# A two-block transformer step on one core: gate columns, row maxima and sums of the second block in another form, the last halves by positions, output by two queues

## What is computed

```python
h = rms_norm(x, norm1_w) * (1.0 + scale) + shift
proj = h @ w_in + b_in
(q, k, v, o, z_a, i_pre, f_pre, u, b_gate, c_gate, z_b, g_a, g_b) = split(proj)
# eight heads: i_pre and f_pre are 8 columns each ("gate columns")
b = cumsum(log_sigmoid(f_pre)); d = b[l] - b[s] + i_pre[s]      # causal
m_row = max(running maximum of d, ...)                          # "row maxima"
scores = (q @ k.T) * dk**-0.5 * exp(d - m_row)
num = scores @ v; den = sum(scores)                             # "sums"
h_a = num / max(|den|, exp(-m_row))
...
x = x + gate * (merged @ w_out)
return rms_norm(x, normf_w)
```

## Time and profile before

| | before |
|---|---|
| median of 3 runs | 2489.23 us (2488.03 to 2490.27) |
| the profiled execution, its own time | 2487.7 us |
| its span | 2485.9 us |
| PE busy | 2379.5 us, 96% |
| VectorE (DVE) busy | 1672.4 us, 67% |
| ScalarE (ACT) busy | 1136.7 us, 46% |
| POOL busy | 93.6 us, 4% |
| mean granted clock of PE | 0.981 |

### The profile page before, as it was taken

One profiled execution on the slowest core, in us unless ns is written; L12 is line 12 of the kernel. 1 busy time (PEld: TensorE's weight loads), 2 busy tenths in 40 slices (PEclk: granted clock), 3 DMA queues, 4 the chain that ended last, 5 costly groups with the idle time before them and its releaser, 6 DMA issues.

```text
span 2485.9 us, 27431 instructions
## 1 busy us (share of the span) xinstructions
PE 2379.5 (96%) x10764; PEld 1965.3 (79%) x10764; DVE 1672.4 (67%) x1807; ACT 1136.7 (46%) x1486; POOL 93.6 (4%) x60
## 2 busy tenths in 40 slices
PE   3689999989999999999979999999999999999997
PEld 3577787868888888888868888888888888888886
DVE  7888898968888888755565455565556555555565
ACT  3345566554444444444463434443445544444453
POOL 1000000001111111200000000000000001000000
PEclk8899999989999999999989999999999999999999
DMA  9978889959899999855544655555566657655553
GB/s 330 356 280 312 273 281 348 348 191 339 322 335 325 331 325 324 293 197 199 193 147 164 200 182 190 180 182 183 195 202 203 208 198 247 208 194 189 189 189 110
DMA packets 255668, 600.52 MB, mean 242 GB/s; under 512 B 12680, under 2 KB 13000, under 8 KB 249024
## 3 DMA queue, kind: packets, MB, share of 16 engines
q1 hardware_dynamic: 252640, 589.48, 68.1%
q0 software_dynamic: 2912, 9.44, 1.2%
HBM read 596.74 MB, written 2.13 MB: 241 GB/s over the span
## 4 chain that ended last, share of the span: by engine, by line
PE 89%; DVE 6%; DMA 2%; ACT 2%; issue 1%; SPq 0%; DVEq 0%; ACTq 0%
PE PS L1185 19%; PE PS L1210 19%; PE PS L1211 18%; PE PS L1216 18%; PE PS L1190 10%; DVE BIAS L1655 3%; DMA RAW<-in_w_in 1%; DVE LO L1637 1%; ACT HI L688 1%; DMA RAW<-in_w_ada 1%; PE PS L1307 1%; PE PS L1570 1%; PE PS L1333 0%; PE PS L1516 0%; PE PS L1199 0%
## 5 line engine op out<-in xcount | busy, mean ns | idle before, releaser
L1637 DVE TENSOR_TENSOR LO<-RAW,HI 128x1024 fp32r<-128x1024 f32 x808 | 1021.0, 1269 | 723.3 <-ACT HI L688 722.3
L688 ACT ACTIVATE HI<-RAW 128x1024 fp32r<-128x1024 f32 x808 | 854.3, 1059 | 1228.7 <-PE PS L1216 738.2
L1210 PE MATMUL PS<-HI,XH 128*128 128x512 f32 x2176 | 868.1, 399 | 11.0 <-ACT HI L688 6.5
L1211 PE MATMUL PS<-HI,XL 128*128 128x512 f32 x2176 | 853.4, 392 | 0.0
L1216 PE MATMUL PS<-LO,XH 128*128 128x512 f32 x2176 | 585.9, 391 | 0.6 <-DVE LO L1637 0.6
L1210 PEld LDWEIGHTS PS<-HI,XH 128*128 128x128 f32 x2176 | 412.0, 189 | 101.7 <-ACT HI L688 11.4
L1216 PEld LDWEIGHTS PS<-LO,XH 128*128 128x128 f32 x2176 | 410.7, 189 | 88.5 <-DVE LO L1637 1.7
L1211 PEld LDWEIGHTS PS<-HI,XL 128*128 128x128 f32 x2176 | 412.1, 189 | 83.1 <-issue 1.0
L1655 DVE SCALAR_TENSOR_TENSOR BIAS<-RAW,CACT,BIAS 128x1024 f32<-128x1024 f32 x270 | 346.4, 1283 | 10.5 <-DMA RAW<-in_w_ada 3.1
L1185 PE MATMUL PS<-HI,XH 128*128 128x512 f32 x1056 | 327.7, 392 | 1.1 <-DVE R L1707 1.1
L1185 PE MATMUL PS<-HI,XL 128*128 128x512 f32 x1056 | 326.1, 390 | 0.0
(11 more groups left out here) (283 smaller groups left out, 994.0 us busy)
## 6 DMA issues: line engine op xcount, KB each, us to landing
RAW<-in_w_in SPq DMA_DIRECT2D x208, 1024.0 KB, 5.1
RAW<-in_w_ada SPq DMA_DIRECT2D x112, 1024.0 KB, 5.8
RAW<-in_w_gate SPq DMA_DIRECT2D x88, 512.0 KB, 4.5
RAW<-in_w_up SPq DMA_DIRECT2D x88, 512.0 KB, 5.5
RAW<-in_w_down SPq DMA_DIRECT2D x44, 1024.0 KB, 4.8
RAW<-in_w_ada SPq DMA_DIRECT2D x64, 512.0 KB, 6.5
RAW<-in_w_out SPq DMA_DIRECT2D x32, 1024.0 KB, 5.3
RAW<-in_w_proj_b SPq DMA_DIRECT2D x16, 1024.0 KB, 5.1
```

The costliest lines, as they stand in the source:

```text
L688: act.activation(HI[:, (it["half"] + hf) % HLS, :], RAW[:, it["slot"], hf * 1024:(hf + 1) * 1024], ACT.Copy).then_inc(s.hi_ready, 1)
L1210: pe.matmul(PS[:, bank + u, :], XH[:, 2 * n + kk, rows], hi, start=start and kk == 0, stop=False)
L1211: pe.matmul(PS[:, bank + u, :], XL[:, 2 * n + kk, rows], hi, start=False, stop=False)
L1637: dve.tensor_tensor(LO[:, slot, :], RAW[:, it["slot"], hf * 1024:(hf + 1) * 1024], HI[:, slot, :].bitcast(F32), ALU.subtract).then_inc(s.l ...
```

## The change

It has five parts, none of which alters the result.

1. Gate columns with operands exchanged: the 16 columns are stationary, 256 positions move, the result lies as rows [16 x 256]. The bias is added per partition by VectorE into ROWG, PE's turn goes, and rows 8 to 15 reach partitions 0 to 7 by a DMA of POOL. VectorE waits for it in `gate_rows_out`.
2. Row maxima: ROWM goes to DRAM, and eight broadcasts of POOL's queue bring each row to all partitions (MAXB); the product with SEL and the load of SEL go.
3. Sums: V2 holds 257 columns per head, the last of them ones, so that the same product gives the sum; the product with ones goes.
4. The last two halves take the first positions through both, then the second; `leave` and the squares follow position by position; the first positions' output goes in two pieces by SP, the second's by ScalarE's queue, and the norm's weight is multiplied in ahead of the root.
5. Small loads: positions and frequencies behind the first w_ada chunk, lambdas and masks behind the arrival of X. The row wait at the two section starts moves into `turn_pair` for pairs 4 and later.

```diff
@@ sync: start
-            sp.dma_start(POSI[:], positions[0]...).then_inc(s.pos_in, 16)
-            sp.dma_start(INV, k_inv.to_broadcast([P, 96])).then_inc(s.pos_in, 16)
...
                     if it["j"] == 0:
+                        sp.dma_start(POSI[:], positions[0]...).then_inc(s.pos_in, 16)
+                        sp.dma_start(INV, k_inv.to_broadcast([P, 96])).then_inc(s.pos_in, 16)
                         sp.dma_start(X[:], x[0]...).then_inc(s.x_in, 16)
@@ sync: end
+            for n in range(2):
+                sp.wait_ge(s.out_ready, n + 1)
+                sp.dma_start(out[0, 0:P, 1024 * n:1024 * n + 1024], X[:, 0, 1024 * n:1024 * n + 1024]).then_inc(s.out_done, 16)
@@ gpsimd
+            pool.wait_ge(s.x_in, 16)
             for n, v in enumerate((lambda_q1, lambda_k1, lambda_q2, lambda_k2)):
                 pool.dma_start(LAMV[:, n, :], v.to_broadcast([P, QKD])).then_inc(s.attn_in, 16)
...
-            pool.dma_start(SEL[0:MH, :, :], k_sel).then_inc(s.m_in, 16)
...
+            pool.wait_ge(s.if_ready, 1)
+            pool.dma_start(ROWF, ROWG[MH:2 * MH, :]).then_inc(s.f_rows, 16)
+            pool.wait_ge(s.sum_m, 1)
+            pool.dma_start(max_dram, ROWM).then_inc(s.max_out, 16)
+            pool.wait_ge(s.max_out, 16)
+            for n in range(MH):
+                pool.dma_start(MAXB[:, n, :], max_dram[n:n + 1, :].to_broadcast([P, S])).then_inc(s.max_in, 16)
@@ scalar: end
+            act.wait_ge(s.rstd_ready, 2)
+            act.wait_ge(s.x_normf, 4)
+            for n in range(2):
+                v = X[:, 1, 1024 * n:1024 * n + 1024]
+                act.activation(v, v, ACT.Copy, scale=RSTD[:, 1:2]).then_inc(s.last_ready, 1)
+                act.wait_ge(s.last_ready, n + 1)
+                act.dma_start(out[0, P:S, 1024 * n:1024 * n + 1024], v).then_inc(s.out_done, 16)
@@ tensor
                 if n >= 4:
                     pe.wait_ge(s.pair_out, 8 * t + n - 3)
+                    pe.wait_ge(s.rows_normed, 4 + 3 * t)
...
-            pe.wait_ge(s.rows_normed, 4)
...
-            pe.wait_ge(s.rows_normed, 7)
...
-                    for u in range(NT):
-                        rows = slice(u * P, (u + 1) * P)
-                        for n, (a, b) in enumerate(((XH, WIFH), (XH, WIFL), (XL, WIFH))):
-                            m = pe.matmul(PS[:, 4 + u, 0:16], a[:, k, rows], b[:, k, :], ...)
+                    for n, (a, b) in enumerate(((WIFH, XH), (WIFH, XL), (WIFL, XH))):
+                        m = pe.matmul(PS[0:2 * MH, 4, 0:S], a[:, k, :], b[:, k, :], ...)
...
-                pe.matmul(PS[:, 6, 0:S], SEL[0:MH, n, :], ROWM, start=True, stop=True, skip_group_check=True)\
...
-                for out_ps, rhs in ((PS[:, 6, 256:512], lambda a: V2[:, a, n * MV:(n + 1) * MV]),
-                                    (PS[:, 5, 384 + u:385 + u], lambda a: ONES[:, 0:1])):
-                    for a in range(u + 1):
...
+                for a in range(u + 1):
+                    lhs = PTM[:, u * P:(u + 1) * P] if a == 0 else PTM[:, 256:384]
+                    m = pe.matmul(PS[:, 6, 0:MV + 1], lhs, V2[:, a, n, :], start=a == 0, stop=a == u)
...
+                if h == HALVES_2 - 2:
+                    narrow(sec, h, n, bank_of(g), False, False, (0,))
+                    narrow(sec, h + 1, n + 1, bank_of(g), False, True, (0,)).then_inc(s.first_rows, 1)
+                narrow(sec, h, n, bank_of(g), n == 0, n == 7, (1,) if h >= HALVES_2 - 2 else range(NT))
@@ vector
-                dve.tensor_tensor(GATE_T, PS[:, 4:6, 0:16], B_IF.unsqueeze(1).to_broadcast([P, NT, 16]), ALU.add)\
+                dve.tensor_scalar(ROWG, PS[0:2 * MH, 4, 0:S], B_IF, None, ALU.add).then_inc(s.if_ready, 1)
+                dve.memset(V2[:, :, :, MV:MV + 1], 1.0)
...
-                dve.wait_ge(s.ms_done, n + 1)
-                dve.tensor_tensor(WX[:, 0:256], PS[:, 6, 0:256], MASKM[:, 0:256], ALU.add)
+                dve.tensor_tensor(WX[:, 0:256], MAXB[:, n, :], MASKM[:, 0:256], ALU.add)
...
+                if g == GROUPS_2 - 1:
+                    cols = slice(1536, 2048)
+                    for u in range(NT):
...
+                        dve.tensor_tensor(POST2[:, 1, u], y[:, u, :], GG2[:, cols], ALU.mult).then_inc(s.group_out, 1)
+                        dve.wait_ge(s.group_out, left(g) + u)
+                        dve.tensor_tensor(X[:, u, cols], X[:, u, cols], POST2[:, 1, u], ALU.add).then_inc(s.rows_2, 1)
+                    return
...
+            last_columns(0)
             dve.wait_ge(s.sq_2, 8)
             link(dve.tensor_reduce(SQ, SQ2, AX.X, ALU.add))
             dve.tensor_scalar(MEANSQ, SQ, 1.0 / D, EPS, ALU.mult, ALU.add).then_inc(s.ms_ready, 1)
+            last_columns(1).then_inc(s.x_normf, 1)
             dve.wait_ge(s.root_ready, 6)
+            dve.reciprocal(RSTD, ROOT).then_inc(s.rstd_ready, 1)
...
+            for n in range(2):
+                v = X[:, 0, 1024 * n:1024 * n + 1024]
+                dve.tensor_scalar(v, v, RSTD[:, 0:1], None, ALU.mult).then_inc(s.out_ready, 1)
```

More of the change, by code:

```diff
@@ L305, in build @@
           norm1_w_2, w_ada_2, b_ada_2, w_in_2, b_in_2, conv_w_2, headnorm_w_2, w_proj_a_2, w_proj_b_2,
-          w_out_2, normf_w_2, k_ident, k_inv, k_mask_a, k_mask_b, k_mask_m, k_sel, out):
+          w_out_2, normf_w_2, k_ident, k_inv, k_mask_a, k_mask_b, k_mask_m, out):
     secs = make_plan()
@@ L406, in build @@
         QK2 = region(0, NT, 2048)
-        V2 = region(4096, NT, 2048)
-        YT = region(8192, NK, S)
-        CZ = region(12288, NT, 512)
-        UC = region(13312, 2, NT, 512)
-        BG = region(15360, NT, 512)
-        MASKM = region(16384, 384)
-        SEL = region(16768, MH, P)
-        ROWM = region(17792, S)[0:MH, :]
-        QKT = region(18048, 512)
-        WX = region(18560, 384)
-        PTM = region(18944, 384)
-        ROWB, ROWR, ROWE, ROWF, ROW0, ROW1 = (region(13312 + S * n, S)[0:MH, :] for n in range(6))
-        WIF = region(15360, NK, 16)
-        OT = region(12288, 2, NT, 512)
-        GAB = region(12288, NT, 4096)
+        V2 = region(4096, NT, MH * (MV + 1)).rearrange("p u (n e) -> p u n e", e=MV + 1)
+        YT = region(8208, NK, S)
+        CZ = region(12304, NT, 512)
+        UC = region(13328, 2, NT, 512)
+        BG = region(15376, NT, 512)
+        MASKM = region(16400, 384)
+        MAXB = region(16784, MH, S)
+        WX = region(18832, 384)
+        PTM = region(19216, 384)
+        ROWM = region(19600, S)[0:MH, :]
+        QKT = region(19856, 512)
+        ROWB, ROWG, ROWE, ROWF, ROW0, ROW1 = (region(13328 + S * n, S)[0:MH if n != 1 else 2 * MH, :] for n in range(6))
+        ROWR = ROWG[0:MH, :]
+        WIF = region(15376, NK, 16)
+        OT = region(12304, 2, NT, 512)
+        GAB = region(12304, NT, 4096)
         HAT = lambda k: QK2[:, k % 4 // 2, 512 * (k // 4) + S * (k % 2):512 * (k // 4) + S * (k % 2) + S]
@@ L1512, in gate_columns @@
                 for k in (2 * pair, 2 * pair + 1):
-                    for u in range(NT):
-                        rows = slice(u * P, (u + 1) * P)
-                        for n, (a, b) in enumerate(((XH, WIFH), (XH, WIFL), (XL, WIFH))):
-                            m = pe.matmul(PS[:, 4 + u, 0:16], a[:, k, rows], b[:, k, :], start=k == 0 and n == 0,
-                                          stop=k == NK - 1 and n == 2)
+                    for n, (a, b) in enumerate(((WIFH, XH), (WIFH, XL), (WIFL, XH))):
+                        m = pe.matmul(PS[0:2 * MH, 4, 0:S], a[:, k, :], b[:, k, :], start=k == 0 and n == 0, stop=k == NK - 1 and n == 2)
                 if pair == 7:
                     m.then_inc(s.if_done, 1)
-            def gate_turn():
-                pe.wait_ge(s.if_ready, 1)
-                for g in range(2):
-                    for u in range(NT):
-                        m = pe.transpose(PS[0:MH, 6, g * S + u * P:g * S + (u + 1) * P], GATE_T[:, u, 8 * g:8 * g + 8],
-                                         IDENT[:])
-                m.then_inc(s.if_t, 1)
             def row_turn():
@@ L1585, in quarter_turn @@
                         at = S * (kk % 2) + u * P
[L1586 to L1587 removed]
+                        m = pe.transpose(PS[:, 4 + kk // 2, at:at + P], src(u, kk), IDENT[:])
                 return m
@@ L1615, in beside @@
                     wait(pe, s.mt_ready, i)
-                    quarter_turn(i, GAB).then_inc(s.merge_t, 1)
+                    quarter_turn(lambda u, kk: GAB[:, u, (4 * i + kk) * P:(4 * i + kk + 1) * P]).then_inc(s.merge_t, 1)
             for h in range(HALVES_2):
@@ L2202, in leave @@
                 elif g < CONV:
-                    dst = V2[:, :, 512 * (g - V_AT):512 * (g - V_AT) + 512]
+                    i = g - V_AT
+                    dst = V2[:, :, 2 * i:2 * i + 2, 0:MV]
+                    y, bias = (v.rearrange("p u (n e) -> p u n e", e=MV) for v in (y, bias))
                 elif g < Z_AT:
@@ L2304, in constants @@
            for n in (HD // 2, QKD // 2)]
-    sel = np.zeros((MH, MH, P), np.float32)
```

(4 more changed lines are left out.)

79 lines of the change are left out of this document (35 added, 44 removed).

## The result

The changed kernel takes **2465.64 us** (median of 4 runs, 2463.34 to 2466.05) against 2488.63 of the kernel before in runs beside it: ratio 0.991, 95% interval 0.9892 to 0.9929. Later on, beside further runs of before, it took 2465.12, ratio 0.9904 (0.9887 to 0.992). The forecast was 2470.9 with a range from 2462 to 2480: right in sign and in range, 5 us too slow.

A forecast was written before the change was run, and what follows sets the result against it. TensorE (PE), 89% of the chain, was taken as the bound. Gains of 12.9 us of PE work, 2.2 row waits, 2.5 tail and 0.7 start sum to 18.3 us, giving 2470.9 us, range 2462 to 2480.

The forecast's parts named there:

- Gate columns: Second block, 8 halves: six products of 256 columns replace twelve of 16; gain 4.2 us, bounds 3.1 and 5.5.
- Gate turn: Second block: PE's turn of the gate result goes, the row move by POOL costs nothing; gain 0.5 us.
- Maxima: Second block's eight heads: the product against SEL goes, 0.58 us a head; gain 4.6 us, between 3.4 and 5.0.
- sums: Second block's eight heads: the denominator's ones-products go, 0.45 us a head; gain 3.6 us, between 1.3 and 4.5.
- Row waits: Feed-forward and second-block starts: PE's idle 1.08 and 1.12 us before the last rows goes; gain 2.2 us, ends 1.1 and 6.
- the high end: Section starts: gapless turns bring the clock's rise forward to the first product, some 2 us more each; 6 us in all.
- Tail: Behind the last product: first output issued at 4.0 instead of 6.6 us; gain 2.5 us, ends 1.5 and 3.0.
- Start: Kernel start: small loads moved away, mostly into full DMA; gain 0.7 us, ends -1.0 and 4.1.
- The start did not pay in full: Rival at the start: early X brings the first w_in early, 4.1 us instead of 0.7, 2467.5 us; chance 0.08.
- the gate products took 0.117 us and not 0.43: Rival in the second block: gate products at plain fp32 rate, 0.43 us each, loss of 9.8 us, 2484.9; chance 0.04.
- PE's shorter list: Rival in the second block: half of the 12.9 us becomes waits for HI or LO around heads, 2477.4; chance 0.05.
- the weight stream was not blocked: Rival in the second block: POOL's eight broadcasts hold up the weight stream, PE stops 40 us, 2511; chance 0.03.

The follow-up runs named there:

- dead products: Changed kernel plus, behind each head, the old row-of-maxima product (2474.12 us) or, in another run, the old three denominator products (2471.93 us), read by nobody.
- one queue: Changed kernel with all four 512 KB outputs issued by SyncE in the order they are ready, none by ScalarE's queue: 2466.22 us.
- the row waits back: Changed kernel with the two section-start row waits back behind the fourth pair of turns: 2468.28 us, ratio to before 0.9926.
- the loads later: Changed kernel with POOL's lambda loads waiting for the second high part and its masks for the twentieth: 2460.83 us, ratio to before 0.9899.

## Why the prediction was right, and where its terms were off

- **Gate columns**: 5.2 for 4.2. The six products have no step before or behind them; their cost of 0.70 to 0.72 us a half is all but the lower bound, half of the 512-column price (0.68).
- **Gate turn**: 0.5, as said. The moved rows made nobody wait (VectorE has no wait for DMA there).
- **Maxima**: 6.3 for 4.6, beyond my upper bound of 5.0, and **sums**: 5.2 for 3.6, beyond 4.5. The step that failed is the same in both: my upper bounds, 0.63 and 0.56 us a head, are the odd products' own time alone. The step from the pieces ahead to the odd product I left with those pieces, as if it stayed when the product goes, and I let a step behind come back. The dead products show that the odd product brings the step ahead of it: 0.17 and 0.18 us go with it.
- **Row waits**: 2.2 said, 5.3 in the pair of traces, 3.8 in the experiment that puts them back. The idle part was nearly right (2 times 1.3 for 2 times 1.1). At the second block the rest, 1.1, is the clock's rise, which I had named for the high end and then laid aside. At the feed-forward the pair has 1.6 more that the experiment does not show; it is the late rise in the trace of before, perhaps chance. I leaned on the Trainium skill, "TensorE: Matmul & The Clock Gate", Part 4: PE-mode transpose, by which transposes do not count as busy time. Here they do: in four section starts (3.0, 3.2, 3.4 and 3.6 us behind the first turn) the clock rose with nothing but turns behind the idle time, and turns alone held it at 1.00 for 11 us. The row I cited for it, turns of 3.8 us that did not raise the clock, was one execution with the idle gap behind them.
- **Tail**: 2.3 for 2.5. Both outputs came within 0.1 us of the sum, the end 0.25 later than it. "Output by two queues" is no part of it.
- **Start**: 0.7 said, -0.3 in the traces and -0.6 by the mean of eight executions (against one of before). The mechanism was right (moved into full DMA, not removed), the size of one edit was not: position and frequency loads cost 2.0 where I had them inside a balance of 0.9, since behind the first chunk they hold up the queue in which X follows. ScalarE's first high part came at 42.30 and not near 41.3.
- **Not in the sum**: the unchanged work from the first product to the feed-forward took 475.2 to 481.2 us in the thirteen traces without added turns in that part, and falls of the clock between 60 and 400 us go with it. Some come behind waits: in the changed kernel one of 3.4 us stands behind a wait of 2.1 us at 386 to 388, where the trace of before has a wait of 1.8 and no fall. By my estimate it costs 1.7 us: the products in it start 0.43 us apart instead of 0.23. Others stand at full busy time, near 294 us in most traces and near 234 in seven of them (clock 0.75 from 232 to 236 us with one queue, 1.00 in the changed kernel). The trace with one queue, which has the longest way, has a mean clock of 0.94 from its first product to 510 us; that with the row waits back, 475.4, has 0.96. That all of the 2.5 us lost in the changed kernel's trace comes from such falls is likely and not shown.

Of the rivals none came. The start did not pay in full, the gate products took 0.117 us and not 0.43, PE's shorter list shortened the time (17.0 us in the stretches of the second block's products), and the weight stream was not blocked.

PE work 17.0, starts 5.3, tail 2.3, start -0.3, the stretch before the feed-forward -2.5, and -0.15: 21.7 us. That the forecast's 18.3 came within 3.4 of it is in part luck: four terms were too small, by 7.4 us together (gate columns, maxima, sums, row waits), and they met 3.5 us of losses that it did not have, the start and the stretch before the feed-forward.

## To carry to other kernels

When a product of an odd form is removed, compare the whole half around it with a plain one: here the step ahead of it went too. At the waits tried here (7 to 12 us) idle TensorE time cost twice, once as itself and once as half speed behind it. Turns that nobody reads kept the clock up; they paid behind the third w_ada wait, where TensorE's work is the bound, and not at the section starts, where a split is. A small load moved away from a busy start should go behind the last transfer that the start waits for. Between two large ones of the same queue it cost 2.0 us; ahead of all of them it put the first chunk back by 1.0 and the first product not at all.

## What was not expected of the hardware

- Turns (transposes against IDENT) raise TensorE's clock and hold it: in four section starts it rose 3.0 to 3.6 us behind the first of them, before any product, and it stayed at 1.00 through 11 us of little else.
- The clock also fell to 0.50 for 3.4 us with TensorE busy without a gap, from a moment between 282 and 297 us in twelve of the fourteen traces. The two without it there, the row waits back and the loads later, have the shortest ways from the first product to the feed-forward (475.4 and 475.15 us) of the thirteen without added turns in that part. What stands directly ahead in the changed kernel is a run of short work, turns, scores and w_ada's sums, sixteen products of one column. Its timeline there, then a window behind it:

```profile
289.36 1.13 PE L1350 MATMUL PS<-R 64*128 64x256 f32 x4
290.42 1.95 PE L1324 MATMUL PS<-ONES,BIAS 128*128 128x1 f32 x16
292.23 0.48 PE L1226 MATMUL PS<-HI,XH 128*128 128x512 f32 x1
...
292.00:294.00 2.00, 2.00 (x11) 0.90 1.06 388
```

  That this work is the cause was not tried.
- A load of 1 KB and one of 48 KB, issued on the weights' queue ahead of X, left 21 GB/s of some 400 for a microsecond and cost the first product 2.0 us (two traces, where equal starts differ by 0.6).
- Runs of one kernel differ by up to 6 us, those of before by up to 8, and 2 us at the start, plain in the traces, could not be told in the times.
